# Experts stage of a decoder layer: finer column widths, half blocks on two column halves, and one list of branches per width

## What is computed

```
def moe_ffn(h, router_w, router_b, w_gate_up, b_gate_up, w_down, b_down):
    logits = (t @ router_w + router_b)
    top_logit, top_idx = lax.top_k(logits, TOP_K)
    ...
    def expert_block(args):
        tok, e = args
        gu = t[tok] @ w_gate_up[e] + b_gate_up[e]
        gate = jnp.minimum(gu[:, 0::2], SWIGLU_LIMIT)
        up = jnp.clip(gu[:, 1::2], -SWIGLU_LIMIT, SWIGLU_LIMIT)
        act = (up + 1.0) * gate * jax.nn.sigmoid(SWIGLU_ALPHA * gate)
        return act @ w_down[e] + b_down[e]
```

## Time and profile before

| | before |
|---|---|
| median of three runs | 3850.54 us |
| span of the profiled execution | 3852.9 us (no time beside its span is given for it) |
| TensorE busy | 3178.5 us, 82% of the span |
| stage of the experts (first to last matmul) | 1660 to 3722 us of the span |
| mean granted TensorE clock in that stage | 0.98 of full speed |

### The profile page before, as it was taken

One profiled execution on the slowest core, in us unless ns is written; L12 is line 12 of the kernel. 1 busy time (PEld: TensorE's weight loads), 2 busy tenths in 40 slices (PEclk: granted clock), 3 DMA queues, 4 the chain that ended last, 5 costly groups with the idle time before them and its releaser, 6 DMA issues. The chain is left out here.

```text
span 3852.9 us, 47314 instructions
## 1 busy us (share of the span) xinstructions
PE 3178.5 (82%) x16004; PEld 2380.5 (62%) x16005; DVE 1244.9 (32%) x3431; ACT 601.8 (16%) x1419; POOL 183.0 (5%) x188
## 2 busy tenths in 40 slices
PE   4337776699999599579999999999999998999960
PEld 1114443577777356367777776867777786876740
DVE  1114444066666256322222122222222221221214
ACT  0001111045554133111000000110111010000100
POOL 0000000000000001110000000000000000000000
PEclk7568887599999799589999999999999999999985
DMA  2331111332200321085644566665775564646707
GB/s 97 124 119 47 47 36 44 64 95 74 74 12 4 129 61 44 28 314 203 217 170 167 180 239 217 214 215 188 261 272 211 203 237 162 224 154 233 257 12 261
DMA packets 313556, 569.46 MB, mean 148 GB/s; under 512 B 83374, under 2 KB 118574, under 8 KB 312344
## 3 DMA queue, kind: packets, MB, share of 16 engines
q1 hardware_dynamic: 273416, 524.37, 40.2%
q0 software_dynamic: 21152, 38.50, 3.0%
q10 hardware_dynamic: 18832, 4.33, 0.5%
HBM read 528.99 MB, written 72.19 MB: 156 GB/s over the span
## 5 line engine op out<-in xcount | busy, mean ns | idle before, releaser
L1593 PE MATMUL ps<-xT_e,wg 128*128 128x128 f32 (+2 forms) x8192 | 1270.0, 319 | 75.9 <-issue 39.1
L1593 PEld LDWEIGHTS ps<-xT_e,wg 128*128 128x128 f32 x8192 | 1227.9, 201 | 131.8 <-issue 56.6
L1604 PE MATMUL ps<-wd,aT 128*128 128x512 f32 x1504 | 650.8, 592 | 0.0
L1604 PEld LDWEIGHTS ps<-wd,aT 128*128 128x128 f32 x1504 | 283.3, 190 | 344.4 <-issue 344.4
L1549 DVE TENSOR_SCALAR gg<-ps,bias 128x128 f32<-128x128 f32 (+2 forms) x256 | 101.4, 396 | 782.8 <-PE ps L1593 782.7
L1562 DVE COPY ys_e<-ps 128x1024 f32<-128x1024 f32 x47 | 56.2, 1222 | 670.8 <-PE ps L1604 670.8
L1526 ACT ACTIVATE ss<-gg 128x128 f32<-128x128 f32 (+2 forms) x256 | 88.7, 346 | 956.9 <-DVE gg L1549 956.5
L452 PE MATMUL ps<-w_in,hT_a 128*128 128x430 f32 x512 | 188.0, 529 | 0.0
L1526 ACT ACT_TABLE_LOAD x32 | 41.1, 1283 | 879.2 <-issue 879.2
L800 ACT ACTIVATE sc<-sc,nm 128x640 f32<-128x640 f32 (+15 forms) x256 | 161.4, 633 | 70.7 <-DVE nm L833 70.7
L452 PEld LDWEIGHTS ps<-w_in,hT_a 128*128 128x128 f32 x512 | 98.2, 193 | 87.8 <-issue 87.4
(11 more groups left out here) (287 smaller groups left out, 2644.3 us busy)
## 6 DMA issues: line engine op xcount, KB each, us to landing
wg<-in_w_gate_up SPq DMA_DIRECT2D x128, 2048.0 KB, 7.8
wd<-in_w_down SPq DMA_DIRECT2D x128, 1024.0 KB, 4.8
yr<-d_ys SPq DMA_DIRECT2D x8, 2048.0 KB, 7.2
skew<-d_rev SPq DMA_DIRECT2D x18, 512.0 KB
w_in<-in_w_in SPq DMA_DIRECT2D x1, 6880.0 KB
d_strip<-strip SPq DMA_DIRECT2D x9, 512.0 KB, 2.7
x_a<-in_x POOLq DMA_DIRECT2D x8, 512.0 KB, 7.3
kn<-d_kn SPq DMA_DIRECT2D x8, 512.0 KB
```

The source lines that it names most:

```text
L1593: mm = pe.matmul(ps[:, j % 2, half * PASS:half * PASS + w], wg[:, j // 2, k, c0:c0 + 255:2], xT[:, k, 0:w], start=(k == 0), stop=(k == KD ...
L1604: mm = pe.matmul(ps[:, 2 + 2 * b + h, :], aT[:, j, b * P:(b + 1) * P], wd[:, c, j % 2, h * 512:(h + 1) * 512], start=(j == 0), stop=(j == ...
```

## The change

- Gate-up, activation and sigmoid are compiled for nine widths, 128 to 256 in steps of 16 (`by_width`), picked by nested `If`s; a pass runs at its row count rounded up to 16, and at least 128.
- The down projection and the copy to `ys` are picked apart from that (`by_blocks`): two full blocks; one full and one of up to 64 rows; one full; one of up to 64. A block of up to 64 rows is multiplied with only 64 stationary columns, the first half of the output to PSUM partitions 0 to 63 and the second to 64 to 127 of the same bank, one after the other for each j.
- TensorE waits for `s_up` (VectorE has read both halves) instead of `s_a` before it overwrites a bank.
- If the next pass has no second block, it is not turned, nor copied to `xT`.
- `ys` is cleared once at the start, not per missing block; GpSimd waits for both blocks of `ys` before the first scatter.

```diff
@@ stage_experts
+        WIDTHS = tuple(range(P, PASS + 1, 16))
+
+        def by_width(eng, n, body, widths=WIDTHS):
+
+            if len(widths) == 1:
+                body(widths[0])
+                return
+            half = len(widths) // 2
+            with eng.If(n > widths[half - 1]):
+                by_width(eng, n, body, widths[half:])
+            with eng.Else():
+                by_width(eng, n, body, widths[:half])
+
+        def by_blocks(eng, n, body):
...
                         def scatter(nb):
+                            pool.wait_ge(s_y, CREDIT + 2 * i + 2)
+                            hold(pool, e.pool_passed)
                             for b in range(nb):
-                                pool.wait_ge(s_y, CREDIT + 2 * i + 1 + b)
-                                hold(pool, e.pool_passed)
...
-                                ch(dve.tensor_scalar(u, ps[:, j % 2, PASS:PASS + w], bias[:, 8 + j:9 + j], LIMIT, ALU.add, ALU.min))
+                                dve.tensor_scalar(u, ps[:, j % 2, PASS:PASS + w], bias[:, 8 + j:9 + j], LIMIT, ALU.add, ALU.min).then_inc(s_up, 1)
+                                dve.wait_ge(s_up, CREDIT + JD * i + j + 1)
...
+                        def gate_up(w):
                             for j in range(JD):
                                 if j % 2 == 0:
                                     pe.wait_ge(s_wg[j // 2], CREDIT + 16 * i + 16)
-                                pe.wait_ge(s_a, CREDIT + JD * i + j - 1)
+                                pe.wait_ge(s_up, CREDIT + JD * i + j - 1)
...
-                            turn_rows(i + 1)
-                            pe.wait_ge(s_a, CREDIT + JD * i + JD)
-                            pe.wait_ge(s_y, CREDIT + 2 * i)
+                        by_width(pe, n, gate_up)
+                        with pe.If(rows_left(pe, i + 1) > P):
+                            turn_rows(i + 1, 2)
+                        with pe.Else():
+                            turn_rows(i + 1, 1)
+                        pe.wait_ge(s_a, CREDIT + JD * i + JD)
+                        pe.wait_ge(s_y, CREDIT + 2 * i)
+
+                        def down(rows):
                             for c in range(NCH):
                                 pe.wait_ge(s_wd[c], CREDIT + 16 * i + 16)
-                                for b in range(nb):
-                                    for h in range(2):
+                                for b, r in enumerate(rows):
+                                    if r == P:
+                                        for h in range(2):
...
+                                    else:
                                         for j in (2 * c, 2 * c + 1):
+                                            for h in range(2):
+                                                mm = pe.matmul(ps[h * r:(h + 1) * r, 2 + 2 * b, :], aT[:, j, b * P:b * P + r], wd[:, c, j % 2, h * 512:(h + 1) * 512],
+                                                               start=(j == 0), stop=(j == JD - 1))
                                 mm.then_inc(s_down, 1)
-                        by_size(pe, n, body)
+                        by_blocks(pe, n, down)
```

More of the change, by code:

```diff
@@ L1424, in stage_experts @@
         s_wd = [sem(f"e_wd{c}") for c in range(NCH)]
-        s_gu, s_g, s_sig, s_a, s_down, s_y, s_sd, s_dch = (sem("e_" + n) for n in
-            ("gate_up", "gate", "sigmoid", "act", "down", "y", "scatter_done", "dve_chain"))
+        s_gu, s_g, s_up, s_sig, s_a, s_down, s_y, s_sd, s_dch = (sem("e_" + n) for n in
+            ("gate_up", "gate", "up", "sigmoid", "act", "down", "y", "scatter_done", "dve_chain"))
         def rows_left(eng, i):
@@ L1435, in first_slot @@
             return eng.value_load(e.plan[0:1, bass.ds(4 * i + 1, 1)], min_val=0, max_val=NE * CAP - PASS)
-        def by_size(eng, n, body):
+        WIDTHS = tuple(range(P, PASS + 1, 16))
[9 more added lines that the diff above has]
+        def by_blocks(eng, n, body):
             with eng.If(n > P):
                 with eng.If(n > P + P // 2):
-                    body(2 * P, 2)
+                    body((P, P))
                 with eng.Else():
-                    body(P + P // 2, 2)
+                    body((P, P // 2))
             with eng.Else():
-                body(P, 1)
+                with eng.If(n > P // 2):
+                    body((P,))
+                with eng.Else():
+                    body((P // 2,))
         with nc.Block() as block:
@@ L1557, in body, with evict, turn_rows @@
                             ch.end()
+                        by_width(dve, n, activate)
+                        def evict(rows):
                             dve.wait_ge(s_sd, CREDIT + i)
-                            for b in range(2):
-                                if b < nb:
-                                    dve.wait_ge(s_down, CREDIT + NCH * i + NCH)
+                            dve.wait_ge(s_down, CREDIT + NCH * i + NCH)
+                            for b, r in enumerate(rows):
+                                if r == P and len(rows) == 2:
                                     dve.tensor_copy(ys[:, b, :].rearrange("p (c n) -> p c n", c=2), ps[:, 2 + 2 * b:4 + 2 * b, :]).then_inc(s_y, 1)
                                 else:
-                                    dve.memset(ys[:, b, :], 0.0).then_inc(s_y, 1)
-                        by_size(dve, n, body)
+                                    halves = [ps[0:r, 2 + 2 * b, :], ps[r:2 * r, 2 + 2 * b, :] if r < P else ps[:, 3 + 2 * b, :]]
+                                    for h in range(2):
+                                        done = dve.tensor_copy(ys[0:r, b, h * 512:(h + 1) * 512], halves[h])
+                                        if len(rows) == 1 or h == 1:
+                                            done.then_inc(s_y, 1)
+                        by_blocks(dve, n, evict)
             @block.tensor
             def _(pe):
-                def turn_rows(i):
+                def turn_rows(i, nb):
                     pe.wait_ge(s_x, 32 * i + 32)
@@ L1573, in turn_rows @@
                         for kk in range(2):
-                            for b in range(2):
+                            for b in range(nb):
                                 c = 2 * k + kk
```

38 lines of the change are left out of this document (22 added, 16 removed).

## The result

The changed kernel takes 4044.18 us, the median of four runs (4043.26 to 4046.18); the kernel before, run beside it, takes 3848.89 us. The ratio is 1.0517, with a 95% interval of 1.0495 to 1.054: slower by 195 us, where 4087 us was forecast in a range of 3880 to 4215.

What follows compares the result with a forecast made beforehand. TensorE was taken to bound the experts' stage. From 3852.9 us, 270 us of savings and removed waits go and 506 us of code fetching and lost clock come, giving 4089, then 4087 us at the runs' median; range 3880 to 4215 us.

Steps and rivals of the forecast that it cites:

- narrower gate-up: Gate-up matmuls: row counts rounded up to 16 mean fewer columns in wider passes, saving 107 us.
- column halves: Down projection: matmul pairs for blocks of up to 64 rows overlap fully, saving 68 us (bounds nothing and 75).
- bank free once read: Inside gate-up: TensorE no longer waits for the sigmoid before overwriting a PSUM bank, saving 37 us.
- no turn of a missing block: Turning of the next pass's rows: 17 of 32 turns lose half, about 1.1 us each, saving 19 us.
- old "issue" wait, counted anew: TensorE's existing "issue" waits: 39 us taken off, because such waits are counted again among the added costs.
- stops before gate-up: Before each gate-up, TensorE's jumps to code not held cost 5.8 us each, less the sequencer's lead, adding 415 us.
- jump to the tail: From a wider copy's end to the tail: 13 jumps miss at 4.7 us, less a lead, adding 27 us.
- clock behind the stops: TensorE's matmuls after a stop run at a lower clock: 2.3 us lost at each of 28 stops, adding 64 us.
- rival 3: Down projection or turning: column halves don't overlap, or a wait for the last `aT` replaces turning; 4155 us, inside the forecast.
- Rival 1: TensorE's jumps: code is there in time, so only the savings stand; 3580 us, chance 0.13.
- rival 2: TensorE's jumps cost only 3.3 to 3.6 us each, like the cheap one before; 3840 to 3870 us, chance 0.05.
- Rival 4: VectorE's spread nine copies also miss, reaching the first group 2 to 5 us late; up to 4200 us, chance 0.1.

Runs made afterwards that it cites:

- e2: The changed kernel with its nine copies and branches kept, but each copy computing 128, 192 or 256 columns as before the change: 4135.38 us, ratio 1.0757 to the kernel before.
- g2: The kernel before the change, with TensorE waiting for `s_up` instead of `s_a` before it overwrites a PSUM bank: 3799.51 us, ratio 0.9882.
- e1: The changed kernel with gate-up, activation and sigmoid compiled for three widths (128, 192, 256) instead of nine: 3799.61 us, ratio 0.9891 to the kernel before.
- e3: The kernel before, with five never-executed gate-up copies at each pass's head and five at its end, on TensorE alone: 4304.77 us, ratio 1.1198.
- e4: The changed kernel with its nine copies, but all branches of the width choice at the head, before the first copy: 3727.37 us, ratio 0.9697 to the kernel before.
- f3: The nine-copy kernel with branches at the head, with ScalarE and TensorE loading the next row count early in the pass: 3732.47 us, ratio 0.9703 to the kernel before.
- f4: The nine-copy kernel with branches at the head, with two blocks always turned and copied, no count loaded and no branch: 3691.63 us, ratio 0.9592 to the kernel before.
- h1: Four widths (128, 144, 208, 256), branches at the head, two blocks always turned, plus 20 never-executed matmuls in the 256-row copy: 3663.94 us, ratio 0.9541 to the kernel before.
- h2: Four widths (128, 144, 208, 256), branches at the head, two blocks always turned, plus 64 never-executed matmuls in the 256-row copy: 3762.98 us, ratio 0.9796 to the kernel before.
- f1: The nine-copy kernel with branches at the head, with TensorE again waiting for `s_a` before overwriting a PSUM bank: 3801.64 us, ratio 0.9861 to the kernel before.
- f2: The nine-copy kernel with branches at the head, with blocks of up to 64 rows projected down as full ones: 3776.08 us, ratio 0.9798 to the kernel before.

## Why the prediction held, step by step

| step | forecast, us | measured, us | from |
|---|---|---|---|
| narrower gate-up | -107 | -106 | gate-up in e2 and in the change |
| column halves | -68 | -46 | down projections, with their clock, before and in the change |
| bank free once read | -37 | -59 | 37 of waits (before), 22 of clock (g2) |
| no turn of a missing block | -19 | +17 | from gate-up to down, without the jump |
| old "issue" wait, counted anew | -39 | -39 | |
| stops before gate-up | +415 | +334 | waits of L1622 |
| jump to the tail | +27 | +34 | waits of L1604 |
| clock behind the stops | +64 | +56 | gate-up in e2 and in g2 |
| sum | +236 | +191 | the spans differ by +190 |

The measured column is made of sums over the traces, with gate-up and the down projections taken from the first to the last matmul of each pass and the waits inside gate-up apart.

The mechanism was right and was shown. The code, not the computation, costs 336 us (e1, e2); it does so when it is never executed (e3) and mostly not when the branches stand together (e4). The number of slow branches was foreseen as some 110 and is 114. The queue q8 reads 246 times more than before, where some 300 were foreseen. That the time came within 43 us of the forecast is partly luck: the stops were put 81 us too dear, and the savings 37 us too high. The range's lower end, 3880 us, also lies above the 3870 that the prediction itself gives for a cheap jump; the result is far from both.

**The price of a jump was mis-sized.** "5.8 us" for a branch at the head or in the choice was read from two of the three rows, and they are dear ones. Over the whole stage before, the seven slow loop branches (L1581) have a mean of 5.81 us, but the eleven in the choice (L1439, L1440) have 4.98; together that is 5.30. The seven at a body's end (L1442) have 3.44 and were priced apart, at 3.6. In the change the 98 ahead of gate-up have a mean of 4.98. With this, the prediction's own chain gives 4 x 4.98 + 1.4 - 7.6 = 13.7 us for a narrow pass behind a narrow pass, where 13.94 and 15.25 were measured; with 5.8 it gave 17.0. The prediction counts some 97 such jumps, so 0.82 us less for each is 80 us, about the whole difference between forecast and measured stops. The rows of before would have given 48 us of it.

Two smaller errors beside it partly cancel. The prediction halved the sequencer's lead for seven narrow passes behind half blocks (20.8 us each). That is right where the pass before had only a half block: passes 1 and 9 waited 19.05 and 20.23 us. The other five, behind passes that mix full and half blocks, waited 8.80 to 14.08 us. Against that, pass 0 waited 21.84 us, where 11.6 was put down.

**The short turn went the other way.** Nothing was put down for the load of the next count and its branch, only for what they save. On ScalarE they stand between the last sigmoid and the copy that TensorE waits for. The timeline of the change in such a turn:

```profile
2784.36 0.31 ACT L1542 ACTIVATE ss<-gg 128x128 f32<-128x128 f32 x1 [3.46 <-DVE gg L1569]
2785.33 0.66 ACT L1523 ACTIVATE xT_e<-ps 128x256 f32<-128x256 f32 x2 [0.66 <-issue]
2785.77 0.71 PE L1604 MATMUL ps<-ident_e,xg 128*128 128x128 f32 x4 [1.39 <-ACT xT_e L1523]
```

and before, in a full turn:

```profile
2754.46 0.31 ACT L1526 ACTIVATE ss<-gg 128x128 f32<-128x128 f32 x1 [3.46 <-DVE gg L1549]
2754.68 1.06 ACT L1507 ACTIVATE xT_e<-ps 128x512 f32<-128x512 f32 x2
2755.31 1.14 PE L1576 MATMUL ps<-ident_e,xg 128*128 128x128 f32 x8 [0.40 <-ACT xT_e L1507]
```

The half turn needs half the transposes, and then stands 1.39 us where the full one stood for 0.40. f3 moved the load away and gained nothing; on TensorE it then lay in the chain before gate-up, which is the longer wait, though f3's text also lies otherwise and the cause is not isolated. Only f4, without load and branch, gains, 36 us. In the traces of e4 and f4 the jump to the turning gives 10 of these, the rest of the way to the down projection 7, and the down projections 13: they are at half clock for 29 us in e4 and for 4 in f4. As f4's text is also shorter, some of the 36 may be due to that, after h1 and h2.

**The early release** was counted right in its waits (37 us, all but 3 of it gone in g2) and left out the clock behind them, 22 us, which f1 beside e4 shows once more. That VectorE would be late anyway was right too, and small: e1 shows 9.8 us and e4 7.3 us of waits for `uu`. The whole worth lies between 46 us (g2, median) and 74 (f1 and e4, medians).

**Narrower gate-up.** Windows of L1622 alone at widths 144 and 208 answer to the earlier trace rows:

```profile
2190.00:2214.00 24.00, 24.00 (x198) 24.00 (x198) 1.00 0.60 214
1790.00:1830.00 40.00, 40.00 (x229) 40.00 (x228) 1.00 0.49 168
```

24.00 / 198 is 121 ns and 40.00 / 229 is 175 ns, where 123 and 175 were interpolated. The term came as forecast, 106 for 107 us. Only 91 of it show in the time of e2 against the change, because some of it comes back as waits behind the shorter gate-up.

**Column halves overlap.** In a pass at width 144 full and half blocks alternate:

```profile
2228.91 1.94 PE L1645 MATMUL ps<-wd,aT 128*64 128x512 f32 x8
2230.77 3.70 PE L1640 MATMUL ps<-wd,aT 128*128 128x512 f32 x8
2234.41 1.94 PE L1645 MATMUL ps<-wd,aT 128*64 128x512 f32 x8
```

The two records of a pair start 7 ns apart in the trace. From start to start eight half records take 1.86 us and eight full ones 3.64, so pairs run side by side, and a change of form costs some 0.2 us: 3.64 less 8 x 0.426 is 0.23, and 1.86 less 4 x 0.426 is 0.16. By f2 beside e4 the halves save 72 us of down projection, which is the forecast. Against before, only 46 us are left, because down projections now run at half clock in places. Behind the turning in pass 0, the window from 1704 to 1707 us reads

```profile
1704.00:1707.00 3.00, 2.86 (x8) 1.03 (x10) 0.53 1.06 413
```

at a granted clock of 0.53, with the short turn's waits of 1.4 and 0.6 us just ahead. The halves are not the cause, since full blocks of f2 do the same. Two windows of its down projection in pass 29, at its start and later:

```profile
3511.40:3514.40 3.00, 3.00 (x4) 1.44 (x5) 0.52 1.02 399
3520.00:3523.00 3.00, 3.00 (x8) 1.33 (x7) 1.00 0.76 276
```

Summed over the stage, down projections are at half clock for 0 us before, 35 in the change and 42 in f2. f2 needs 24 us more for the same down matmuls as before (655.6 against 631.8). What stands ahead of them is new: the short turn's waits and the jump to the tail. The rule of the Trainium skill (TensorE: Matmul & The Clock Gate, "The mechanism") that a weight load overlaps matmuls in flight only when the row group differs would have made this part of rival 3 true; in these rows all pairs share the row group and still take half the time (1.86 against 3.64 us), which agrees with its section "Measured speedup vs the span model".

**The rivals.** Rival 1, the code is there in time, and rival 2, a jump at 3.3 to 3.6 us, both fall with the branches: 98 slow ones ahead of gate-up at 4.98 us in the mean. The cheap kind exists, but elsewhere: ten of the 14 jumps from a copy's end took 3.3 to 3.5 us, the other four 5.3 to 6.1. Of rival 3, the wait in place of the shorter turn came true, and the missing overlap did not. Rival 4 falls: VectorE's branches stay at 56 ns in the median. Why its nine copies cost it nothing was not tried; the other instruction queue, q14, did read 190 times where it had read 4 times before.

**How much is held.** The Trainium skill (Runtime: NRT & Kernel Launch, "Instruction fetch mechanics") has blocks of 256 instructions and room for 2048. The shift by 256, which brought the stop back one transpose away, agrees with the first. For the second, the prediction's count, seven pieces held and nine not, lies on both sides of the eight blocks that this room makes; no run here sets it closer. Its other sentence, that only two pages are kept, stays contradicted by the earlier trace rows, where the way back to the head took 0.215 to 0.232 us.

## What to carry to other kernels

Before compiling a loop's body in more variants, count its instructions and the pieces that one turn of the loop touches: a jump to a piece that isn't held costs 4.85 us here, and four in a row are far more than the lead of 7.6 us. Put all branches of a choice together and ahead of the copies; here this one line was worth 317 us. Then look for a stop that always falls behind the same instruction, since a shift of the text may remove it, and compare variants only at equal text, or with several shifts. And look at the clock behind each wait that goes or comes: here 37 us of waits carried another 22 us with them.

## What was not expected of the hardware

- Never-executed instructions inside a loop cost 460 us (e3), and shifting the text by 80 instead of 256 instructions changes the time by 99 us (h1, h2), with the same instructions executed.
- A slow branch costs 4.85 us in the mean: 4.98 ahead of gate-up (3.54 to 7.60) and 4.03 at a copy's end (3.31 to 6.10).
- The wait before gate-up grows when the matmuls before the loop's end get faster: passes behind nothing but a half block waited 19.05 and 20.23 us, other narrow passes with four slow branches 13.6 to 15.3, and f2's slower down projections gave 18 us of their 72 back.
- The same program text of TensorE had 25 slow branches before and 22 in g2, with 39.1 and 25.3 us of "issue" before gate-up, so which jumps are slow is not fixed by the text alone.
